# Two half projection units, each cut in two around a linear step, in the triangular loop of a hybrid recurrent kernel

## The reference, cut to what matters

```python
(g_q, g_k, ..., d_qkv, ..., h_q, h_f, h_i, h_g) = jnp.split(h @ w_in[li], offs, axis=-1)
# the delta rule, per chunk of 64 tokens: a unit lower triangular system
m = jnp.where(strict, jnp.einsum('bhid,bhjd->bhij', kb, kc) * gam, 0.0)
tmat = eye + m
u = lax.linalg.triangular_solve(tmat, vb, left_side=True, lower=True, unit_diagonal=True)
w = lax.linalg.triangular_solve(tmat, kb * jnp.exp(gcum)[..., None], ...)
# the two linear groups, per chunk: attention with a decay for each key column
decay = jnp.where(m3, jnp.exp(jnp.where(m3, diff, 0.0)), 0.0)
att = jnp.einsum('bhid,bhjd,bhijd->bhij', qc, kc, decay)
```

## Time and profile before

| | |
|---|---|
| median of 3 runs | 1425.25 us |
| lowest and highest | 1421.78 and 1433.71 us |
| the profiled execution | 1424.59 us, span 1422.8 us |
| TensorE busy | 1252.5 us (88% of the span) |
| VectorE, ScalarE, GpSimd busy | 633.0, 397.0, 472.6 us (44%, 28%, 33%) |
| granted TensorE clock, mean | 0.931 of full speed |

### The profile page before, as it was taken

The page is one execution under the profiler, slowest core; times in us unless marked ns, Lnnn a source line. Parts: engine busy times, 40 slices in busy tenths (PEclk is TensorE's granted clock), DMA queues, the critical chain, the costliest instruction groups (busy, mean ns, idle before and its releaser), DMA issues. The chain is left out here.

```text
span 1422.8 us, 32185 instructions
## 1 busy us (share of the span) xinstructions
PE 1252.5 (88%) x13694; PEld 955.2 (67%) x13694; DVE 633.0 (44%) x1372; ACT 397.0 (28%) x832; POOL 472.6 (33%) x398
## 2 busy tenths in 40 slices
PE   7988899989999999999998999977844999998960
PEld 6878689879879978978987987766732333333320
DVE  2749752445156246335435534544343322222228
ACT  2243134234224223323423422421110122221214
POOL 1616572372155236228227337223001111111100
PEclk9999999999999999999999998977856999999985
DMA  9887537735834844862783562490066989999968
GB/s 271 265 220 242 170 103 245 235 105 174 286 123 142 276 150 127 262 204 97 248 259 105 179 210 92 131 139 20 6 264 266 354 333 389 417 416 416 410 249 320
DMA packets 217735, 317.28 MB, mean 223 GB/s; under 512 B 15332, under 2 KB 187952, under 8 KB 209000
## 3 DMA queue, kind: packets, MB, share of 16 engines
q1 hardware_dynamic: 205176, 277.51, 58.2%
q10 hardware_dynamic: 5792, 20.78, 4.3%
q0 software_dynamic: 6624, 16.92, 3.1%
HBM read 295.45 MB, written 27.01 MB: 227 GB/s over the span
## 5 line engine op out<-in xcount | busy, mean ns | idle before, releaser
L1563 PE MATMUL psum<-arena 128*128 128x256 f32 (+3 forms) x1536 | 307.1, 355 | 4.2 <-issue 4.2
L1563 PEld LDWEIGHTS psum<-arena 128*128 128x128 f32 x1536 | 255.7, 194 | 33.4 <-issue 5.0
L2408 PE MATMUL psum<-arena 128*64 128x512 f32 (+1 forms) x832 | 167.9, 608 | 6.7 <-DMA arena<-in_exp_w 6.7
L1246 DVE COPY_PREDICATED arena<-arena,psum 128x128 f32<-128x128 int32 x280 | 85.3, 305 | 129.1 <-PE psum L1741 122.2
L1559 PE MATMUL psum<-arena 128*128 128x128 f32 x1152 | 138.3, 280 | 2.9 <-DVE arena L1102 1.5
L1559 PEld LDWEIGHTS psum<-arena 128*128 128x128 f32 x1152 | 133.8, 195 | 5.7 <-issue 5.2
L672 POOL TENSOR_TENSOR arena<-arena 128x768 f32<-128x768 f32 (+1 forms) x32 | 59.1, 1848 | 201.3 <-ACT arena L900 201.3
L2408 PEld LDWEIGHTS psum<-arena 128*64 128x64 f32 (+1 forms) x832 | 51.9, 133 | 105.5 <-issue 103.2
L1828 PE MATMUL psum<-arena 128*128 128x256 f32 x512 | 116.4, 386 | 0.8 <-ACT arena L977 0.8
L1828 PEld LDWEIGHTS psum<-arena 128*128 128x128 f32 x512 | 97.9, 194 | 14.6 <-ACT arena L977 1.2
L2250 POOL DMA_INDIRECT y_d<-arena x23 | 23.0, 1002 | 219.0 <-DVE arena L2349 219.0
(11 more groups left out here) (402 smaller groups left out, 2031.0 us busy)
## 6 DMA issues: line engine op xcount, KB each, us to landing
arena<-in_w_in SPq DMA_DIRECT2D x96, 1024.0 KB, 6.2
arena<-in_exp_w SPq DMA_DIRECT2D x96, 1024.0 KB, 16.8
arena<-in_w_out SPq DMA_DIRECT2D x32, 1024.0 KB, 5.7
arena<-in_w_in SPq DMA_DIRECT2D x24, 512.0 KB, 5.4
arena<-y_d SPq DMA_DIRECT2D x16, 512.0 KB, 11.0
arena<-in_x_prompt ACTq DMA_DIRECT2D x15, 512.0 KB, 6.1
arena<-in_w_in SPq DMA_DIRECT2D x8, 576.0 KB, 4.5
arena<-in_w_in SPq DMA_DIRECT2D x8, 560.0 KB, 4.2
```

What stands on the lines that cost most here:

```text
L1246: ins = v.copy_predicated(h3(att_b)[:, h:h + 2, :], b3(q_mask[4 * half + j], 2, 64), new)
L1563: ins = mm(b[:, 0:n], hT[:, c, :], w[:, c, 0:n], start=(c == 0), stop=(c == KC - 1))
L2408: ins = mm(bank[2 + q % 2][at:at + width, :].rearrange("p (m n) -> p m n", m=2), xT[q % 2][:, c, at:at + width], w13[n % NB][:, :, c, :], ...
```

## The change

The second half of unit 14 (level 1) and the first half of unit 15 (level 2) stood behind the second linear step of their level. Each is now two parts of two matmuls: the first directly behind `TU`, ahead of the linear step, and the second where the half stood. Levels 0, 3, 4 and 5 are as they were, and so is the sequence of every engine but TensorE.

```diff
@@ order, a list written once
         order.append(("TU", level))
+        if level and b:
+            order.append(("part", level))
         for _ in range(b):
             order.append(("lin", n))
             n += 1
@@ unit(t, k, part)
-                if part != 1:
+                part = part or (0, KC)
+                if part[0] == 0:
                     chunk(pe, "in", t, k)
...
-                    for c in range(KC) if part is None else range(4 * part, 4 * part + 4):
+                    for c in range(*part):
                         ins = mm(b[:, 0:n], hT[:, c, :], w[:, c, 0:n], start=(c == 0), stop=(c == KC - 1))
-                if part != 0:
+                if part[1] == KC:
                     ins.then_inc(step("unit_done"), 1)
@@ the loop over order, on TensorE
-                    elif what == "unit":
-                        unit(n, spot(n, LOOP_UNIT + m // 2), m % 2)
+                    elif what in ("unit", "part"):
+                        lo, hi = KC // 2 * (m % 2), KC // 2 * (m % 2) + KC // 2
+                        if what == "part":
+                            hi -= KC // 4
+                        elif ("part", m) in order:
+                            lo += KC // 4
+                        unit(n, spot(n, LOOP_UNIT + m // 2), (lo, hi))
```

## The result

The changed kernel took 1415.8 us (median of 7 runs, 1413.23 to 1419.8), the kernel before 1425.38 us (7 runs, 1421.78 to 1433.71). The ratio is 0.9927 with a 95% interval from 0.9899 to 0.9954: faster by 0.7%, so inside the 1% that the forecast called the same, and 9.6 us between the medians, where 6.4 were forecast. The profiled execution of the changed kernel took 1419.8 us with a span of 1418.0; it is the slowest of the seven, and the profiled one before lay near its median, so the two profiles lie only 4.8 us apart.

A forecast was written before the change was run, and what follows sets the result against it. TensorE's own row and its pauses were taken to bound tiles 0 to 6. Per level, the pause of 0.65 us less 0.20 for a switch saves 0.46; 14 levels give 6.4 us, so 1418.5 us, range 1412 to 1427.

The forecast's parts named there:

- The bound and the place: Tiles 0 to 6: TensorE's own row sets the time; 14 waits for VectorE's puts, at linear steps 3 and 5, go.
- What the wait costs: Linear step behind `TU`, levels 1 and 2: start to start 1.51 us with the wait, 0.86 without, so 0.65 us.
- The price of the second switch: Small matmuls to full array once more per level: 0.20 us, bounds 0 and 0.40; a part takes 1.06 us.
- The covers: Later waits keep room: linear step 3 0.41 us, next `P` 1.2, step 6 0.58; unit 15's chunk and bank cost nothing.
- The pause only moves: Rival: the wait for the puts returns a little later in the tile; time stays at 1424.9 us. Chance 0.06.
- the split is free: Rival: the added switch costs nothing, so 14 x 0.65 = 9.1 us are saved, 1415.8 us. Chance 0.07.
- More pauses for instructions: Rival: denser levels 1 and 2 make instructions late, 6.1 us a pause; two more give 1430.7 us. Chance 0.05.
- The size: Whole kernel: 6.4 us saved, 1418.5 us, range 1412 to 1427 us.
- the sum: `TU` to next `P`, levels 1 and 2: 4.05 us becomes 3.59, saving 0.46 in 14 levels, 6.4 us.

The follow-up runs named there:

- the undivided units: Half units of levels 1 and 2 moved whole ahead of the second linear step, against the kernel before: 1417.35 us, ratio 0.9957.
- the three parts: Changed kernel's split, but level 1's two parts stand ahead of linear steps 2 and 3; against the kernel before 1415.2 us for 1426.5, ratio 0.9921.
- the three comparisons: Changed kernel against the kernel before: first 0.9927, repeated without an edit 0.9937, and both kernels with 32 small matmuls in front 0.9943.
- the second profile of the changed kernel: From the changed kernel run again without an edit, against the kernel before: 1416.5 us for 1425.92, ratio 0.9937.

## Why the prediction was right, and where it was short

- The bound and the place: right. TensorE's row sets the time in tiles 0 to 6, and 14 waits for the puts went.
- What the wait costs, 0.65 us and not the bracket's 0.59: right; with the undivided units the whole of it is won, 4.05 less 3.40.
- The price of the second switch, 0.20 us, taken between 0 and 0.40: right, 1.06 us for the part. The rule of the Trainium skill (TensorE: Matmul & The Clock Gate, Step-by-step: what each phase is for) on loads pulled ahead into the background buffer would have made the part 0.86 us; at this border, small matmuls to full-size ones, the trace disagrees: the parts take 1.06 us in all 14 levels.
- The covers: right, each to 0.01 or 0.02 us (0.57 us of room at step 6 for 0.58; no wait at `P`, at the chunk or at `sums`). "The pause only moves" and "the split is free" are refuted by rows. That the measured median, 1415.8 us, is the very number that the prediction gave for a free split is chance: the part took 1.06 us and not 0.86. Two small slips change nothing: the waits of unit 15 come 1.3 us earlier by the figures given (411.5 for 412.8), not 1.1, and a level of 3.59 us for 4.05 is 11% shorter, which is 13% denser.
- More pauses for instructions, as a way to a slower time: the pauses are there, but the price was too high for most. The 6.1 us are a pause with a fall of the clock; without a fall one cost 1.4 us in tile 1 and 0.6 in tile 4. None came into levels 1 and 2 of the changed kernel, but one more came into level 5, in tile 4. In tile 1 the pause became shorter and the fall of the clock behind it stayed away, in both profiles. The net went the other way from what this rival expected.
- The size: the range held the time, the value of 1418.5 us was 2.7 us too high, and the gain of 6.4 was short of the 9.6 measured. That the range held 1415.8 us is in part luck: it was made wide for the switch and for one pause more or fewer, and the extra gain came by neither in that form. The step that was off is the sum, which had one term: it put the clock and the pauses down as scatter with no direction. Over 19 runs the changed kernel lost 92.7 us with the low clock, the kernel before 97.6 over 81 runs, beside what the waits explain.

What stays open is whether the change causes that second part. For it: two profiles of either kernel, with 2.51 and 1.68 us in tile 1 and a low clock behind, against 1.30 and 1.40 and none; and the 4.9 us over many runs, about four times its standard error. Against it: in tile 6 the same pause of 1.52 us had a clock of 0.79 behind it in one profile of the changed kernel and 1.00 in the other, so the fall varies between executions of one kernel. Against a general effect: the undivided units and the three parts have the same or fewer waits and pauses of 1.31 us without a fall in tile 1 in their profiles, but lose 97.6 and 96.8 us, as much as before. Why TensorE ran dry later against the packet of instructions in tile 1 wasn't settled either. The intervals of the three comparisons all reach to 0.9954 or beyond, so none of them alone excludes 6.4 us (0.9955) clearly; the means of the 19 and the 81 runs lie 10.0 us apart, with a standard error of 1.1 if the runs are independent and the chips alike, which speaks for a second part.

## What to carry to other kernels

Where an engine works through a fixed order, a wait is worth the distance from start to start, not the idle time in brackets, and independent work put in front of it is worth that distance less the cost of one more change of shape; both can be read from neighbouring rows to a hundredth of a microsecond. The smallest piece that reaches the release is enough, and if the work behind has room, the undivided piece saves the change of shape too. A gain of some microseconds in a program of 1.4 ms, whose single runs lie up to 17 us apart, is seen in the timeline at once but in the medians only with many runs; splitting each run by its mean clock made it visible there too.

## What the runs showed of the hardware

TensorE's pauses without a semaphore stand at places of its instruction stream that the count of instructions ahead sets: in tiles 1, 5 and 6 between the same two matmul records in all eight profiles without padding; 128 instructions more in front (32 matmuls) took them from there and put one into tile 3, and 64 in front instead moved the one of tile 5 by 31 records. They lasted 0.3 to 2.6 us in level 5 and the half unit behind it, and one of 1.28 us stood in level 2. Whether one shows depends on the density as well: at one place in tile 4 it cost 0 us in the kernel before, 0.43, 0.79 and up to 1.48 us in the versions with shorter loops. At each a packet of instructions (16 KB) started 2.3 to 2.6 us before TensorE went on, so they are late fetches of instructions as far as the records can show it. The Trainium skill (Runtime: NRT & Kernel Launch, Instruction fetch mechanics) has blocks of 256 instructions and calls the crossing mostly hidden, and here 0.3 to 2.6 us of it were not, several times in an execution.

The clock behind these pauses does not follow their length alone. In tile 1 it stayed full behind 1.30 to 1.40 us in four profiles and behind 1.61 in a fifth; behind 1.68, 1.69 and 2.51 us the mean of 16 us was 0.68, 0.89 and 0.79. In tile 6, behind a pause of 1.52 us each time, it was 1.00 in two profiles, 0.79 and 0.89 in two others. It also fell where no such pause stood, to a mean of 0.83 from 545 to 555 us in the second profile of the changed kernel.
